# Twelve of sixteen modulation units as split products in the prologue of a two-layer diffusion backbone

## What is computed

```
m = silu(cond) @ mod_w[l] + mod_b[l]        # cond is c, and c_ctx for the context; split in six
sh1, sc1, g1, sh2, sc2, g2 = split(m, 6)
rmsnorm(x, g) = x * rsqrt(mean(x*x) + eps) * g
n_lat = rmsnorm(x, norm1_g[0]) * (1 + sc1) + sh1
n_ctx = rmsnorm(ctx, norm1_g[0]) * (1 + csc1) + csh1
q, k, v, xr, gr = split(n_lat @ w_in)       # and the same weights on n_ctx
```

## Time and profile before

| what | us |
|---|---|
| median of three runs | 2296.51 (2292.99 to 2296.66) |
| the profiled execution's own time | 2295.41 |
| span of its profile | 2293.6 |
| PE busy in the span | 2234.5 (97%) |
| last modulation unit issued to PE until done | up to 53.62 |
| first product of the projection | 57.77 |

### The profile page before, as it was taken

The page is one execution under the profiler, slowest core; times in us unless marked ns, Lnnn a source line. Parts: engine busy times, 40 slices in busy tenths (PEclk is TensorE's granted clock), DMA queues, the critical chain, the costliest instruction groups (busy, mean ns, idle before and its releaser), DMA issues.

```text
span 2293.6 us, 27308 instructions
## 1 busy us (share of the span) xinstructions
PE 2234.5 (97%) x10246; PEld 1819.7 (79%) x10246; DVE 1480.8 (65%) x1897; ACT 841.0 (37%) x1396; POOL 1139.1 (50%) x726
## 2 busy tenths in 40 slices
PE   7999999999999999999999899999899999999998
PEld 3788887878778888888888678888688888888886
DVE  5677765854775555558777987665975555555553
ACT  3555546852533333332213522234533333332112
POOL 3222314788545555565443445574365555564340
PEclk9999999999999999999999999999999999999999
DMA  9756558734132222247652122260132222242321
GB/s 344 211 157 172 161 170 202 166 129 138 37 110 83 83 83 83 83 169 259 219 198 96 42 83 74 74 207 10 60 98 89 83 84 83 83 153 92 110 83 74
DMA packets 296942, 282.95 MB, mean 123 GB/s; under 512 B 64783, under 2 KB 242155, under 8 KB 296299
## 3 DMA queue, kind: packets, MB, share of 16 engines
q1 hardware_dynamic: 258747, 257.61, 36.3%
q10 hardware_dynamic: 37488, 21.50, 3.3%
q0 software_dynamic: 576, 2.10, 0.2%
HBM read 226.36 MB, written 57.16 MB: 124 GB/s over the span
## 4 chain that ended last, share of the span: by engine, by line
PE 70%; DVE 6%; POOL 1%; issue 1%; ACT 1%; DMA 1%; DVEq 0%; POOLq 0%; ACTq 0%
PE bank L1102 23%; PE bank L1104 23%; PE bank L1103 23%; DVE act_lo L2138 1%; DVE act_hi L2138 1%; DMA pair_raw<-in_o_w_in 1%; DVE x_rms L2130 0%; PE bank L1145 0%; DVE bank L2049 0%; DVE pair_raw L2115 0%; DVE low_f L2123 0%; POOL slot L1063 0%; PE bank L1129 0%; DVE t_sum L2105 0%; DVE a L2138 0%
## 5 line engine op out<-in xcount | busy, mean ns | idle before, releaser
L2057 DVE SCALAR_TENSOR_TENSOR h<-bank,mods,h 128x512 f32<-128x512 f32 x384 | 287.2, 750 | 260.8 <-PE bank L1104 255.6
L1063 POOL TENSOR_TENSOR slot_lo<-pair_raw,slot_hi 128x512 fp32r<-128x512 f32 x112 | 170.1, 1519 | 282.1 <-ACT slot_hi L1621 282.1
L1063 POOL TENSOR_TENSOR slot_lo<-t_sum,slot_hi 128x512 fp32r<-128x512 f32 x109 | 163.6, 1523 | 158.3 <-ACT slot_hi L1621 158.3
L1063 POOL TENSOR_TENSOR slot<-pair_raw,slot 128x512 fp32r<-128x512 f32 x144 | 233.8, 1644 | 16.0 <-ACT slot L1621 16.0
L2218 DVE TENSOR_TENSOR bank<-bank,p 128x512 f32<-128x512 f32 x53 | 37.0, 698 | 290.6 <-PE bank L1104 290.6
L1102 PE MATMUL bank<-act_lo,slot_hi 128*128 128x512 f32 x436 | 170.8, 392 | 6.6 <-DVE act_lo L2138 5.9
L1621 ACT CAST slot_hi<-pair_raw 128x512 fp32r<-128x512 f32 x112 | 69.0, 616 | 287.8 <-DMA pair_raw<-in_ffn_w_gu 239.1
L1102 PE MATMUL bank<-a,slot_hi 128*128 128x512 f32 x436 | 171.5, 393 | 2.3 <-ACT p L1630 0.8
L1104 PE MATMUL bank<-a,slot_hi 128*128 128x512 f32 x436 | 170.5, 391 | 0.0
L1104 PE MATMUL bank<-act_lo,slot_hi 128*128 128x512 f32 x436 | 169.8, 389 | 0.0
L1103 PE MATMUL bank<-a,slot_lo 128*128 128x512 f32 x436 | 169.7, 389 | 0.0
(11 more groups left out here) (329 smaller groups left out, 5962.2 us busy)
## 6 DMA issues: line engine op xcount, KB each, us to landing
pair_raw<-in_ffn_w_gu SPq DMA_DIRECT2D x88, 512.0 KB, 4.4
mod_in_f<-in_mod_w SPq DMA_DIRECT2D x48, 512.0 KB, 3.7
z_spill<-silu_g SPq DMA_DIRECT2D x88, 256.0 KB, 2.7
mod_in_p<-in_mod_w SPq DMA_DIRECT2D x32, 512.0 KB, 4.7
pair_raw<-in_o_w_in SPq DMA_DIRECT2D x24, 512.0 KB, 3.7
raw<-in_e_w_in SPq DMA_DIRECT2D x20, 512.0 KB, 4.5
low_f<-z_spill SPq DMA_DIRECT2D x40, 256.0 KB, 5.0
a_f<-z_spill SPq DMA_DIRECT2D x18, 512.0 KB, 6.2
```

The lines of the kernel that those rows point to most:

```text
L1063: nc.gpsimd.tensor_tensor(low, from_, high, ALU.subtract).then_inc(s_wlo, 1)
L2057: V.scalar_tensor_tensor(out=dst, in0=bank[:, b, :], scalar=mods[:, gate, m:m + 1], in1=dst, op0=ALU.mult, op1=ALU.add).then_inc(s_hup, 1)
```

## The change

- A modulation unit of `MOD_SPLIT` (1 to 5, 7 to 13) is now a split product. ACT makes its high part (`mod_high`), DVE or, for units 1, 3, 5, 7 and 9, POOL its low part; PE multiplies both with `cond_s`, four columns that hold high and low parts of the two conditionings (four float32r products of 512 columns). The parts lie in weight slots 2 and 3, in turn: the high part of a unit waits until the unit two before it in `MOD_SPLIT` is summed. Units 0, 6, 14 and 15 stay plain float32. The sums have four rows, folded to two in `mod_turn`, now a float32 product with `fold_rows` in place of a transpose.
- Statistics come in three parts: root, reciprocal, diagonals and spread of the first half after the fourth tile, of the second half after the eighth, of the context after the tenth; the first half's `x_rms` stands between the last tile copies on DVE, the second half's between its last four low parts.
- SP's queue: weight unit 0 is loaded behind modulation unit 11, weight units 1 to 3 behind all modulation units; the ring's waits follow the new order of units.
- POOL makes its five low parts first, then splits weight units 0 and 1, and units 2 and 3 after all sixteen modulation units are summed.
- In the first column block the projection's first two products of a k wait for the high part only, the third for the low part; later blocks do not wait at all.

```diff
-        mod_row = at(83, "mod_row", [2, 2, UNIT])
+        mod_row = at(83, "mod_row", [4, 2, UNIT])
+        cond_s = at(81.5, "cond_s", [P, FT, 4], F32R)
+        cond_d = at(82, "cond_d", [P, FT, 4])
+        fold_rows = at(82.25, "fold_rows", [4, 2])
...
+        MOD_TILE = {4: (0,), 6: (1,), 7: (2, 3), 8: (4,), 9: (5,)}
+        MOD_ORDER = tuple(u for tt in sorted(MOD_TILE) for u in MOD_TILE[tt]) + (6, 7, 8, 9, 10, 11, 12, 14, 13, 15)
+        MOD_SPLIT = (1, 2, 3, 4, 5, 7, 8, 9, 10, 11, 12, 13)
+        MOD_POOL = (1, 3, 5, 7, 9)
+        MOD_DVE = tuple(u for u in MOD_SPLIT if u not in MOD_POOL)
+
+        def mod_done(u):
+            return (s_modmm, MOD_ORDER.index(u) + 1)
...
+        def mod_hi(u):
+            return w_hi4[:, 2 + MOD_SPLIT.index(u) % 2, :]
+
+        def mod_lo(u):
+            return w_lo4[:, 2 + MOD_SPLIT.index(u) % 2, :]
...
-                    sp.wait_ge(s_modmm, u - 7)
+                    sp.wait_ge(*mod_done(u - 8))
...
-            for j in range(2):
-                load_unit(j, j, column_unit(w_in, order_p[j]))
             for u in range(8, 2 * FT):
                 load_first_mod(u)
-                if u in (11, 13):
-                    j = (u - 7) // 2
-                    load_unit(j, j % 2, column_unit(w_in, order_p[j]))
+                if u == 11:
+                    load_unit(0, 0, column_unit(w_in, order_p[0]))
+            for j in range(1, 4):
+                load_unit(j, j % 2, column_unit(w_in, order_p[j]))
...
+            steps.run(nc.gpsimd.memset(cond_d[:, :, 2:4], 0.0))
+            nc.gpsimd.tensor_tensor(fold_rows[:], ident[0:4, 0:2], ident[0:4, 2:4], ALU.add).then_inc(s_ident, 1)
...
+            for u in MOD_POOL:
+                pool.wait_ge(s_mhi, MOD_SPLIT.index(u) + 1)
+                nc.gpsimd.tensor_tensor(mod_lo(u), mod_ring[:, u % 8, :], mod_hi(u), ALU.subtract).then_inc(s_mlo_p, 1)
             for j in range(4):
+                if j == 2:
+                    pool.wait_ge(s_modmm, 2 * FT)
                 split(j, j, j % 2)
...
-                        pe.wait_ge(s_norm, 8 * norm + k + 1)
+                        pe.wait_ge(s_nhi, 8 * norm + k + 1)
                     w = (w_hi[:, k * P:(k + 1) * P], w_lo[:, k * P:(k + 1) * P])
-                    mm = product(dst, w, a_hi[:, k, sl], a_lo[:, k, sl], k == 0, k == FT - 1)
+                    low_at = None if norm is None else (s_norm, 8 * norm + k + 1)
+                    mm = product(dst, w, a_hi[:, k, sl], a_lo[:, k, sl], k == 0, k == FT - 1, low_at)
...
+                nth = sum(v // FT == c for v in MOD_ORDER[:MOD_ORDER.index(u)])
+                first, last = nth == 0, nth == FT - 1
+                if u in MOD_SPLIT:
+                    pe.wait_ge(s_mhi, MOD_SPLIT.index(u) + 1)
+                    if u in MOD_POOL:
+                        pe.wait_ge(s_mlo_p, MOD_POOL.index(u) + 1)
+                    else:
+                        pe.wait_ge(s_mlo, MOD_DVE.index(u) + 2)
+                    for a in range(2):
+                        dst, half = bank[0:4, 4 + 2 * c + a, :], slice(a * HALF, (a + 1) * HALF)
+                        pe.matmul(dst, cond_s[:, k, :], mod_hi(u)[:, half], start=first, stop=False)
+                        mm = pe.matmul(dst, cond_s[:, k, :], mod_lo(u)[:, half], start=False, stop=last)
+                else:
+                    pe.wait_ge(s_mod[u % 8], 16 * (u // 8 + 1))
+                    for a in range(2):
+                        mm = pe.matmul(bank[0:4, 4 + 2 * c + a, :], cond_d[:, k, :], mod_ring[:, u % 8, a * HALF:(a + 1) * HALF],
+                                       start=first, stop=last)
                 mm.then_inc(s_modmm, 1)
...
-                    mm = pe.transpose(bank[:, 3, 2 * (c * FT + m):2 * (c * FT + m) + 2], mod_row[:, c, m * P:(m + 1) * P],
-                                      ident[0:2, 0:2])
+                    mm = pe.matmul(bank[:, 3, 2 * (c * FT + m):2 * (c * FT + m) + 2], mod_row[:, c, m * P:(m + 1) * P],
+                                   fold_rows[:], start=True, stop=True)
...
-                if tt >= 4:
-                    if tt == 4:
-                        pe.wait_ge(s_cond, 2)
-                        pe.wait_ge(s_param, 2)
-                    first_mod(tt - 4)
-            pe.wait_ge(s_xp, TT + CT)
-            for u in range(TT + CT - 4, 2 * FT):
+                if tt == 4:
+                    pe.wait_ge(s_ident, 4)
+                    pe.wait_ge(s_cond, 4)
+                    pe.wait_ge(s_param, 2)
+                if tt == 5:
+                    x_spread(0)
+                for u in MOD_TILE[tt] if tt in MOD_TILE else ():
+                    first_mod(u)
+            at_tail = MOD_ORDER[sum(map(len, MOD_TILE.values())):]
+            for u in at_tail:
+                if u == at_tail[2]:
+                    pe.wait_ge(s_xp, TT + CT)
+                    x_spread(1)
+                if u // FT and MOD_ORDER.index(u) == FT:
+                    pe.wait_ge(s_xr, 1)
                 first_mod(u)
-                if u == 9:
-                    pe.wait_ge(s_rstd, 1)
-                    x_spread(0)
-                    x_spread(1)
-                if u == 12:
+                if MOD_ORDER.index(u) == 11:
...
+            def x_diagonals(n):
+                lo, hi = tiles_of(n)
+                act.wait_ge(s_xinv, n + 1)
+                act.wait_ge(s_turn, 2)
+                for j in range(lo, hi):
+                    last = nc.scalar.activation(x_diag[:, j, :], ident[:], ACT.Copy, scale=x_std[:, 2, j:j + 1])
+                last.then_inc(s_rstd, 1)
+
+            def mod_high(u):
+                n = MOD_SPLIT.index(u)
+                act.wait_ge(s_mod[u % 8], 16 * (u // 8 + 1))
+                if n >= 2:
+                    act.wait_ge(*mod_done(MOD_SPLIT[n - 2]))
+                nc.scalar.copy(mod_hi(u), mod_ring[:, u % 8, :]).then_inc(s_mhi, 1)
...
+            HIGH_AT = {5: (1,), 6: (2,), 7: (3,), 8: (4,), 9: (5, 7)}
...
+                    nc.scalar.copy(cond_s[:, :, 0:2], cond[:, :, :]).then_inc(s_cond, 1)
+                    act.wait_ge(s_ident, 4)
+                    nc.scalar.copy(cond_d[:, :, 0:2], cond[:, :, :]).then_inc(s_cond, 1)
+                    x_root(0)
...
+                for u in HIGH_AT[tt] if tt in HIGH_AT else ():
+                    mod_high(u)
+                    if u == 5:
+                        x_root(N_CTX)
+            x_diagonals(N_CTX)
+            for u in MOD_SPLIT[6:9]:
+                mod_high(u)
+            mod_rows(0)
+            for u in MOD_SPLIT[9:]:
+                mod_high(u)
             act.wait_ge(s_const, 1)
             nc.scalar.activation(sp_t[:, 1, :], sp_t[:, 0, :], ACT.Exp, scale=-1.0).then_inc(s_act, 1)
-
-            for c in range(2):
-                act.wait_ge(s_modmm, FT * (c + 1))
-                for a in range(2 - c):
-                    nc.scalar.copy(mod_row[:, c, a * HALF:(a + 1) * HALF], bank[0:2, 4 + 2 * c + a, :]).then_inc(s_modrow, 1)
+            mod_rows(1)
...
+            def mod_low(j):
+                u = MOD_DVE[j]
+                dve.wait_ge(s_mhi, MOD_SPLIT.index(u) + 1)
+                V.tensor_tensor(mod_lo(u), mod_ring[:, u % 8, :], mod_hi(u), ALU.subtract).then_inc(s_mlo, 1)
+
+            LOW_AT = {7: 0, 8: 1}
...
+                if tt in LOW_AT:
+                    mod_low(LOW_AT[tt])
+                if tt == TT - 1:
+                    x_normed(0, range(0, 4))
+                elif tt == TT:
+                    x_normed(0, range(4, FT))
+                    dve.sem_inc(s_xr, 1)
+            x_inverse(N_CTX)
+            mod_low(2)
...
-            for n in (0, 1):
-                dve.wait_ge(s_bc, n + 1)
-                for f in range(FT):
-                    src, _, w, *_ = NORMS[n]
-                    steps.run(V.tensor_tensor(x_rms[:, f, cols(n)], src[:, f, cols(n)], bank[:, SPREAD[n], 0:w], ALU.mult))
-                if n == 1:
-                    mod_first(0)
+            for q in range(4):
+                x_normed(1, range(2 * q, 2 * q + 2))
+                mod_low(3 + q)
+            mod_first(0)
```

71 lines of the change are left out of this document (48 added, 23 removed).

## The result

The changed kernel took 2313.45 us (median of 5, 2309.44 to 2316.25), the kernel before 2295.39 beside it (2292.99 to 2296.66): ratio 1.0075, 95% interval 1.0064 to 1.0086. It is slower, as forecast, but by 18.1 us where the sum had said 10.4, and above the range. The profiled execution took 2315.6 us, 2.2 above that median and 20.2 more than the profiled one of before; its rows follow, in the order in which the prediction used those of before.

The account below looks back on a forecast made before the run. PE was taken to bound the kernel, busy for 97% of the span. Terms of +4.9, +5.9, +0.55 and -0.9 summed to +10.4 us, added to the 2296.5 median: 2307 us, range 2296 to 2311.

Parts of the forecast that it names:

- term one: Modulation stage: low parts queued on DVE and held by POOL's lock make the last unit end later, +4.9 us.
- Term two: Norm stage: POOL's late splits of weight units 2 and 3 lock out DVE, delaying the eighth low part, +5.9 us.
- rival 3: Modulation stage: PE's clock falls after idle gaps, slowing units 13 and 15 and part of group 0; 2311 us, chance 0.15.
- the lower bound: Modulation stage: the low end of term one, if nobody waits, +1.5 us.
- Term three: Second turn after the modulation sums: the float32 product replacing the transpose takes longer on the path, +0.55 us.
- Term four: First projection: PE's 0.9 us lag behind the eighth low part at group 0 is used up, -0.9 us.
- Costed at nothing: Load order, weight units, bias fills and gate loads put at 0; the projection's wait for high parts also gives nothing.
- Rivals 1, 2 and 4: 1: nobody waits, 2298, chance 0.13; 2: faster, 2291, 0.10; 4: split units take no fewer passes, 2308, 0.02.

Follow-up runs that it names:

- e15: The changed kernel, with the first projection's products again waiting for the low part before their first matmul, as in the kernel before; 2312.47 us, ratio 1.0065.
- e1: The changed kernel with POOL's splits of weight units 2 and 3 behind the norm stage's sixteenth low part, and bias fills earlier on SP's queue; 2312.78 us, 1.0068.
- e5: The changed kernel with unread transposes filling PE's four longest gaps in the modulation stage, and 40 more after the second fold; 2308.45 us, ratio 1.0055.
- e18: The changed kernel with the fillings of e5 and the wait for both parts of e15; 2307.43 us, ratio 1.0043.
- e13: The changed kernel with four slots instead of two for the high and low parts of the first ten split units; 2317.78 us, ratio 1.0083.
- e2: The changed kernel with no unit split and POOL's weight splits as before; four rows and folds kept; 2298.97 us, ratio 1.0009.
- e3: The kernel before, with POOL's splits of weight units 2 and 3 made to wait for the sixteenth modulation unit; 2301.37 us, ratio 1.0019.
- e8: The changed kernel with no unit split, and with two rows and transposes in place of four rows and folds; 2302.26 us, ratio 1.0023.
- e6: The kernel before with only the first projection's wait for high parts added and the later column blocks' waits dropped; 2300.83 us, ratio 1.0018.
- e12: The version of e8 with the weight units' loads in the order of the kernel before; 2300.41 us, ratio 1.0012.
- e16: The version of e12 with the wait for both parts, as in the kernel before; 2296.56 us, ratio 0.9992.
- e9: The kernel before with unread transposes in three PE gaps: ahead of the first product, the first gates and the second head; 2298.64 us, ratio 1.0007.
- e10: The version of e6 with the three fillings of e9; 2299.87 us, ratio 1.0007.
- e14: The kernel before with 80 unread transposes on PE ahead of modulation unit 14, as a plain delay; 2307.15 us, ratio 1.0037.

## Why the prediction was right about the direction and short on the size

The sum had +10.4; +18.1 was measured. Two of its steps failed. The first is the last step of term one, the 2.7 us that PE was to need behind unit 13's low part: it took 6.3, with a fold, a spread and two more units to do first, at half clock. The second is the nothing set for the new wait for high parts and for all that comes late in the kernel: the stretch behind the context copy was 5.7 us longer in the profiles. Term two was too high, not too low.

**Term one (+4.9, found +8.8).** The part about DVE's queue held: the last low part was put 40.3 us after the first unit (55.8 - 15.5) and came after 40.6 (57.38 - 16.79), with unit 2's low part at 2.59 us beside POOL's and later ones at 1.43 to 1.97. In e15 it came after 39.5, in e1 after 42.9, so the close hit of one execution is in part luck. What failed is the step behind it, "PE still has units 13 and 15, 2.7 us". PE needed 6.3 (8.2 in e15, 8.0 in e1), since it had not reached unit 13: from 52.38 the fold took 2.81 (1.2 in the sum), the spread 1.22 (nothing in the sum), units 12 and 14 2.0 and 2.9 where 0.91 and 1.77 stood. PE was late on its own account, at half clock in 53.2 to 60.1. This is rival 3 in mechanism, which I had priced at 2311 and for units 13 and 15, while it hit the fold and units 12 and 14. The fillings confirm it. In e5, with part of the fold at half clock, PE needs 4.7 us behind that low part; in e18, with none, 3.2 (54.76 to 57.93), and the whole stage is 4.4 longer than before, close to the 4.9 of the sum. DVE as the pace of the stage is shown by e13, and e2 shows what is left without split units. (A slip in the sum: 55.7 less 1.1 is 54.6, not 55.1; it touches only the lower bound.)

**Term two (+5.9, found +3.3).** The lock between DVE and POOL was right in place, form and cause: `scaled` x2 in 4.51 us, gains 1.37. It was put too high by 2.6. The sum took nearly all of POOL's 6.6 us as lost and only 0.7 off. The splits started at 63.80 with the row copy, and of their time 5.7 us lay behind the start of the gains (66.76 to 72.47). In them DVE did what had taken it 1.3 us before, the gains and two `scaled`; and behind them it ran at 0.64 a low part, with ACT already ahead, without the 1.0 us of idle time. That leaves 3.4. e3 gives the lock's price without any of the rest: +4.4 in its trace. The Trainium skill (SBUF — State Buffer, Who interferes with whom) describes this lock; e8 bears it out down to an operation of eight elements a row, 2.16 us for 0.17.

**Term three (+0.55, found +1.3).** Mis-sized: I counted one record for each transpose and two for each float32 product, which is right, 16 for 8, but took the time of a record from the transposes. It is 0.12 us at full clock (1.91 / 16) against 0.08 (0.62 / 8).

**Term four (-0.9, found -0.2).** PE's lag behind the low parts was not used up: it ran group 0 at half clock until 77.1 and issued the last product at 80.06, 0.7 behind the eighth low part, where it was 0.9 before.

**"Costed at nothing".** Wrong for the wait for high parts. I had written that it gives nothing where the eighth low part ends last; e6 shows that it costs 4.5 us in the kernel before, and e12 with e16 about as much in ratio. In the changed kernel itself it is not clear of the noise (e15: 1.0065 for 1.0075), but for the late parts. What is shown is where an earlier first product goes: ACT's wait for a spill swallows it at the gates, and longer gaps and half clock follow. e9 with e10 speak for these gaps as most of the 4.5; that they are all of it is argued. The order of loads was costed at nothing too: in the changed kernel POOL's splits ran from 47 us on and held up DVE's low parts either way, but e8 against e12 makes it some 2 us where nothing else covers it, with intervals that overlap; the rows show the gains at 2.16 and 0.17. The statistics of the first half at nothing was right (e16).

**Rivals 1, 2 and 4** fell: DVE waits (e3), the gap before the first product grew to 4.65 us, and a split unit takes about 1 us of PE (unit 7: 42.63 to 43.56) for 1.77. For rival 3 I had weighed a sentence of the Trainium skill (TensorE: Matmul & The Clock Gate, Part 4) that transposes don't count as PE work. The runs speak against it for these float32 transposes by the identity: e14's 80 held the clock at 1.00, and e5's kept it up where it had fallen. The clock fell in the changed kernel behind gaps of 3.92 and 2.54 us, and with these filled to 1.32 and 1.85 it did not (e5). It fell a third time around the fold; in e5 it did so with no gap of over 0.65 us between unit 8 and the fold, and in e18 with the same fillings not at all. Why is not shown.

**What stays open.** Why a late part is 2211 in one execution and 2214 in the next, beyond the gaps named; and how much of the 18 us each cause takes in the changed kernel itself, since they overlap. By the runs: clock in the modulation stage about 5 (e5, e18), lock in the norm stage 3 to 4 (e3 and the rows), folds 1.3 on the path, waits for low parts, with the fold and spread that stand among them, the other 4 of that stage's 8.8 (e18), the wait for high parts 1 to 4.

No version beats the kernel before by more than the measurement tells. The best was e16 (early statistics alone), 0.9992 with an interval that touches 1.

## What to carry to other kernels

Before an idle engine's work is halved, list what every other engine must do first for it and where that lands in its queue: twelve split products take some 10 us off PE's own work (0.93 for 1.77 each) and made it wait for DVE, which in turn was shut out by the engine that got the rest of the work. Price the tail behind the last wait at the clock that the gaps before it will bring, not at the one of the trace. And follow a start that comes sooner to the next point where something else (here a spill's landing) sets the time: what it wins may only widen a gap there.

## What the runs showed of the hardware that I had not expected

- An engine pair under the lock slows on both sides: POOL's `w_lo` took 3.24 us instead of 2.34 to 2.36 where DVE's low parts alternated with it (47 to 59 us), besides DVE's 1.43 to 1.97 instead of 1.22.
- A DVE operation on 128x8 took 2.16 us instead of 0.17 beside one POOL operation; a change that moved it by 0.8 us (e2 to e8) switched this on.
- A float32 product with a 4x128 operand as weights costs 0.24 us (two records) for two columns of result. The group of the weight loads in the changed kernel (count | busy, mean ns):

```profile
L1252 PEld LDWEIGHTS bank<-fold_rows,mod_row 4*128 4x128 f32 x32 | 4.6, 224 | 2.2 <-ACT mod_row L1854 1.7 <-issue 0.5
```

- In e9 work that nobody reads raised the mean granted clock to 0.9958 from 0.9948 and did not shorten the run: in the kernel before, PE waits for others in the stretches that it freed from half clock. In e5 the same kind of work gave some 5 us, where PE's own work stood behind the gaps.
